# Six modulation chunks of layer 1: from TensorE products on streamed weights to row sums formed by GpSimd

## The reference

```python
mod = (jax.nn.silu(c) @ w_ada[l] + b_ada[l])[:, None, :]
sh1, sc1, gt1, sh2, sc2, gt2 = jnp.split(mod, 6, axis=-1)
h = modulate(rms_norm(x, g_mix[l]), sh1, sc1)            # h * (1 + scale) + shift
... = split_in(h @ w_in[l])                              # three token mixers and three gates
x = x + gt1 * merge_branches((o_a, o_b, o_c), (ga, gb, gc), w_branch[l], w_out[l])
x = x + gt2 * expert_choice_ffn(modulate(rms_norm(x, g_ffn[l]), sh2, sc2), ...)   # 16 experts
```

## Time and profile before

| | us |
|---|---|
| three runs | 1844.4, 1846.84, 1844.44 |
| median | 1844.44 |
| span of the profiled execution | 1846.3 |
| TensorE busy (share of the span) | 1689.6 (92%) |
| VectorE busy | 771.0 (42%) |
| ScalarE busy | 478.0 (26%) |
| GpSimd busy | 111.4 (6%) |

### The profile page before, as it was taken

One profiled execution on the slowest core, in us unless ns is written; L12 is line 12 of the kernel. 1 busy time (PEld: TensorE's weight loads), 2 busy tenths in 40 slices (PEclk: granted clock), 3 DMA queues, 4 the chain that ended last, 5 costly groups with the idle time before them and its releaser, 6 DMA issues.

```text
span 1846.3 us, 26514 instructions
## 1 busy us (share of the span) xinstructions
PE 1689.6 (92%) x10854; PEld 977.2 (53%) x10854; DVE 771.0 (42%) x1746; ACT 478.0 (26%) x1052; POOL 111.4 (6%) x149
## 2 busy tenths in 40 slices
PE   5999999999998999999898799989999997777866
PEld 2887777777674333333232398877883332222222
DVE  3455556674434233333323665577753222111111
ACT  3324455552223100000000434465441000000001
POOL 1001210000001000000000101300001000000000
PEclk8999999999998999999999999999998999999998
DMA  9532322127778999999999764337899999999996
GB/s 353 154 91 69 106 72 80 35 81 256 251 286 326 409 428 427 428 428 428 427 429 426 271 206 133 96 115 252 282 364 385 426 426 426 426 425 426 426 426 281
DMA packets 152035, 543.83 MB, mean 295 GB/s; under 512 B 10026, under 2 KB 92400, under 8 KB 126700
## 3 DMA queue, kind: packets, MB, share of 16 engines
q1 hardware_dynamic: 149104, 535.35, 74.0%
q0 software_dynamic: 2400, 6.16, 1.2%
q10 hardware_dynamic: 412, 0.64, 0.1%
HBM read 539.13 MB, written 2.98 MB: 294 GB/s over the span
## 4 chain that ended last, share of the span: by engine, by line
PE 68%; DMA 23%; DVE 4%; ACT 2%; SPq 2%; issue 1%; POOL 0%; DVEq 0%; ACTq 0%
PE bank L2158 20%; PE bank L2019 12%; PE bank L2020 11%; PE bank L2021 11%; DMA ring<-in_w_exp_down 8%; DMA ring<-in_w_exp_gate 7%; DMA ring<-in_w_exp_up 4%; DMA spare<-in_w_exp_gate 3%; PE bank L2132 2%; PE bank L2048 2%; PE bank L2071 2%; PE bank L1934 2%; PE bank L2058 2%; PE bank L2187 1%; DMA ring<-in_w_ada 1%
## 5 line engine op out<-in xcount | busy, mean ns | idle before, releaser
L2158 PE MATMUL bank<-ring,XEP 128*32 128x256 f32 (+1 forms) x2384 | 384.9, 617 | 37.1 <-DMA ring<-in_w_exp_gate 20.7
L2019 PE MATMUL bank<-HH,WH 128*128 128x512 f32 (+1 forms) x864 | 312.1, 361 | 5.7 <-DVE HL L1627 4.7
L2020 PE MATMUL bank<-HL,WH 128*128 128x512 f32 (+1 forms) x864 | 300.4, 348 | 0.0
L2021 PE MATMUL bank<-HH,WL 128*128 128x512 f32 (+1 forms) x864 | 299.9, 347 | 0.0
L2158 PEld LDWEIGHTS bank<-ring,XEP 128*32 128x32 f32 (+1 forms) x2384 | 114.1, 130 | 277.5 <-issue 227.8
L1598 DVE TENSOR_TENSOR WL<-ring,WH 128x1024 fp32r<-128x1024 f32 (+1 forms) x172 | 185.0, 1078 | 133.4 <-ACT WH L1362 132.6
L1856 DVE TENSOR_TENSOR X<-X,bank 128x512 f32<-128x512 f32 x184 | 114.0, 682 | 188.2 <-PE bank L2187 100.0
L2019 PEld LDWEIGHTS bank<-HH,WH 128*128 128x128 f32 x864 | 163.8, 190 | 54.0 <-issue 25.9
L1362 ACT CAST WH<-ring 128x1024 fp32r<-128x1024 f32 (+1 forms) x172 | 158.0, 926 | 100.5 <-PE bank L2021 64.7
L2158 PE MATMUL bank<-ring,HIDT 128*32 128x256 f32 (+1 forms) x1232 | 153.6, 481 | 31.3 <-DMA ring<-in_w_exp_down 31.3
L2021 PEld LDWEIGHTS bank<-HH,WL 128*128 128x128 f32 x864 | 163.8, 190 | 21.2
(11 more groups left out here) (244 smaller groups left out, 1955.4 us busy)
## 6 DMA issues: line engine op xcount, KB each, us to landing
ring<-in_w_exp_gate SPq DMA_DIRECT2D x55, 2048.0 KB, 30.9
ring<-in_w_exp_up SPq DMA_DIRECT2D x49, 2048.0 KB, 34.4
ring<-in_w_exp_down SPq DMA_DIRECT2D x48, 2048.0 KB, 36.6
ring<-in_w_ada SPq DMA_DIRECT2D x48, 1024.0 KB, 7.4
ring<-in_w_in SPq DMA_DIRECT2D x40, 1024.0 KB, 6.3
split_slot<-in_w_exp_up SPq DMA_DIRECT2D x8, 2048.0 KB, 29.3
split_slot<-in_w_exp_down SPq DMA_DIRECT2D x8, 2048.0 KB, 33.5
ring<-in_w_in SPq DMA_DIRECT2D x28, 512.0 KB, 5.2
```

What stands on the lines that cost most here:

```text
L2019: mm(t, wh, hi[:, k, 0:b.n], start=k == 0, stop=False)
L2020: mm(t, wh, lo[:, k, 0:b.n], start=False, stop=False)
L2021: last = mm(t, wl, hi[:, k, 0:b.n], start=False, stop=k == b.kk - 1)
L2158: last = mm(out_bank[tw * g:tw * g + tw, 0:nw], stationary(k), w[:, g::G] if spread else w[:, nw * g:nw * g + nw], start=k == 0, stop=k == ...
```

## The change

Chunks 4 to 9 of layer 1 no longer go through the ring and through step "ada". ScalarE's queue loads the halves of a chunk into `row_place`, two places of four rows of 512 columns, which are the upper halves of `X` and of `MRG` (where `spare` lies). GpSimd multiplies each row block by its value of silu(c) (one per partition, for `c` alone; the values for `c_ctx` are not needed here) and adds it to `ROWSUM`, 128 x 512. Then TensorE adds up over the partitions with four products, `ROWSUM` stationary against two columns of ones, which give the result already turned. VectorE copies eight values instead of reducing a bank.

The planner counts the dense steps. The first load stands behind step 16 of layer 1; each chunk's eight form steps begin 28 steps after its load and stand three steps apart; four steps after the last one the chunk counts as formed, and at the end of the next block its products are placed and the next load may follow. The next load waits on ScalarE, half by half, for the sums of the chunk before. The load of `spare` waits for all six chunks and stands behind the window attention, and the loads of chunk 9 are gone from there.

```diff
+ROW_AFTER, ROW_EVERY, ROW_LAG = 28, 3, 4
...
         P.add("done", blk=b)
+        if P.rows_last is not None and P.ticks - P.rows_last[0] >= ROW_LAG:
+            P.deferred.append(P.rows_last[1])
+            P.rows_last = None
...
             P.add("k", blk=atom[1], k=atom[2])
             turn_due(1)
+            form_due()
...
+    def form_due():
+
+        P.ticks += 1
+        if P.rows_due and P.ticks >= P.rows_from and (P.ticks - P.rows_from) % ROW_EVERY == 0:
+            s = P.rows_due.pop(0)
+            s.mods = P.mods
+            P.steps[P.layer].append(s)
+            if not P.rows_due:
+                P.rows_last = P.ticks, s.out_tile
+                P.rows_from = P.ticks + ROW_LAG
+        elif not P.rows_due and P.rows_left and P.ticks >= P.rows_from:
+            rows(P.layer, P.rows_left.pop(0))
...
                     run([("done", head), ("done", b)])
+                    P.rows_left = [5, 6, 7, 8, 9]
+                    rows(l, 4)
...
-        if last:
-            expert_load(Step(o_ready=("ht_ready", 2 * KD)))
...
-            if last:
-                mid = len(sums) // 2
-                now = ((4,), (5, 6), (7,), (8,))[p]
-                sums = sums[:mid] + [("call", ada(l, now[0]))] + sums[mid:] + [("call", ada(l, c)) for c in now[1:]]
             attention("sw", p, info, atoms + sums)
             info = nxt
         o_sw = P.obs
+        if last:
+            expert_load(Step(o_ready=("formed", P.formed)))
...
+                    elif s.kind == "form":
+                        w, cs = row_place[s.k // 4][:, s.k % 4, :], CS[:, s.k, 0:1].broadcast_to((128, 512))
+                        if s.k % 4 == 0:
+                            pool.wait_ge(rows_in[s.k // 4], 16 * (s.n + 1))
+                        if s.k == 0:
+                            pool.wait_ge(mod_ready, s.mods)
+                            link(nc.gpsimd.tensor_tensor(ROWSUM[:], w, cs, ALU.mult))
+                        else:
+                            link(nc.gpsimd.tensor_tensor(w, w, cs, ALU.mult))
+                            add = nc.gpsimd.tensor_tensor(ROWSUM[:], ROWSUM[:], w, ALU.add)
+                            if s.k % 4 == 3:
+                                add.then_inc(formed, 1)
+                                pool.wait_ge(formed, s.formed)
+                            else:
+                                link(add)
...
+                    elif kind == "row_load":
+                        act.wait_ge(ht_ready, KD * DEPTH)
+                        for r in range(2):
+                            if s.before:
+                                act.wait_ge(formed, s.before - 1 + r)
+                            act.dma_start(row_place[r][:], source(("w_ada", s.l, 512 * s.col, 512, 4 * r, 4))).then_inc(rows_in[r], 16)
...
+                    elif kind == "ada2" and s.formed:
+                        pe.wait_ge(formed, s.formed)
+                        for i, out_ in enumerate(s.out):
+                            t = open_tile(out_)
+                            for k in range(4):
+                                cols = slice(k, 512, 4) if i == 0 and s.v in (SH2, SC2) else slice(128 * k, 128 * k + 128)
+                                last = mm(t[:, 2 * k:2 * k + 2], ROWSUM[:, cols], SLOTS[:, 0:1].broadcast_to((128, 2)), start=True, stop=True)
+                            last.then_inc(blk_ready, 1)
```

## The result

| kernel | median, us | runs, us | ratio, 95% interval |
|---|---|---|---|
| before | 1844.42 | 1843.71 to 1846.84 | |
| after | 1884.62 | 1881.43 to 1887.2 | 1.0211, 1.0196 to 1.0225 |

The change costs 40.2 us. The forecast was 1866.8 with a range of 1841 to 1887: the direction and the place are right, the size is a little over half of what was measured. The profiled execution spans 1885.1 us, 38.8 more than the 1846.3 of before. Spans are some 2 us shorter than times (1885.1 belongs to the run of 1887.2), so the profiled execution of before took 2 to 4 us more than the medians of before on this page, and lags read against its trace look better by that than the times do.

A forecast was written before the change was run, and what follows sets the result against it. TensorE was taken to bound the dense stage and the expert stream the end. Terms -7.7 - 2.9 + 12 + 2 + 8 + 11 = +22.4 us on 1844.4 gave 1866.8 us, range 1841 to 1887.

The forecast's parts named there:

- What bounds the kernel: TensorE sets layer 1's dense stage, the expert stream the end; a microsecond on TensorE between 1050 and 1350 moves the end equally.
- Net on TensorE, -7.7: Dense stage: 14.5 us of products and transposes taken off TensorE, 64 records of 6.8 us put on; 7.7 us less.
- The start, -2.9: Layer 1's start: bias masks no longer run beside VectorE's casts and split of the normalised rows; 2.9 us gained.
- The first chunk's wait, 12 + 2: First new product: TensorE waits 12 us for late sums, then loses 2 us to half clock speed.
- the lock: GpSimd and VectorE both wanting SBUF: one stands still until the other's instruction is over; sums progress at about 60%.
- The second chunk in the convolution, 8: 1082 to 1096: GpSimd's 15 instructions put busy VectorE off; TensorE stalls 0 to 12 us, taken as 8.
- Chunks three to six, 11, bounds 0 and 20: 1129 to 1250: 60 GpSimd instructions delay VectorE's weight splits and softmax rows; 11 us, TensorE not waiting for sums.
- The range: Measured time expected between 1841 and 1887 us, 8 in 10; the forecast's own range 1846 to 1885.
- rival 3: Waits feed one another: late masks and starved weight casts make each later chunk cost 8 us; 1888 us, chance 0.13.
- ScalarE's issues at nothing: Twelve DMA issues on ScalarE, 0.37 us each, costed at nothing because ScalarE is idle over a third of every stretch.
- Rivals 1, 2 and 4: 1: all as intended, 1836, chance 0.07; 2: late sums, no lock, 1842, 0.12; 4: stage absorbs it, 1845, 0.04.

The follow-up runs named there:

- e_no_sums: Changed kernel with GpSimd's products and additions left out, except each chunk's first product and two pairs of four-column instructions; 1840.95 us.
- e_pe_free: Changed kernel with all sums in place, but TensorE does not wait for them and its product reads the identity matrix; 1881.46 us.
- e_masks_late: Kernel before, with GpSimd's first bias mask of layer 1 waiting until the split of the normalised rows is over; 1844.72 us.
- e_nobody_waits: e_pe_free with ScalarE's wait gone too: only the first chunk is loaded and its rows are summed again for the others; 1872.14 us.
- e_gpsimd_loads: Changed kernel with products at least 20 dense steps behind the sums, and GpSimd instead of ScalarE issuing the loads; 1888.78 us.
- the chunk at 1098: Second GpSimd chunk, summed 1098 to 1120, in the changed kernel with only chunks 4 and 5 on GpSimd and four on TensorE; 1857.07 us.

## Why the prediction came out as it did

**What bounds the kernel**: right. The loss is in the dense stage, 37.4 of 38.8 us between the profiled executions, and goes to the end within 1.4 us.

**Net on TensorE, -7.7**: e_no_sums has -7.7 - (-2.5) = -5.2 from step 64 to the end of the stage. The products were under-sized: all 64 records are busy for 12.5 us in the changed kernel, and for 11.3 without any wait, not 6.8. A group of eight takes 0.95 us where its weights are adjacent columns of `ROWSUM` (0.12 each, near the 0.107), and twice that where they are every fourth column, as for chunks three to six. At full clock, e_no_sums first and then e_pe_free, which reads the identity matrix in adjacent columns at the same place:

```profile
1142.28 1.91 PE L2060 MATMUL bank<-CONST,ROWSUM 128*128 128x2 f32 x8
```

```profile
1157.44 0.95 PE L2060 MATMUL bank<-CONST 128*128 128x2 f32 x8
```

Four of the eight groups are of that kind. The Trainium skill ("SBUF — State Buffer", the note on SBUF cachelines) says that accesses to the same 16-byte line go at full bandwidth and each that crosses to a new line pays; every fourth fp32 is a new line each time, and the rows agree.

**The start, -2.9**: right by the rows, 3.0 on VectorE and 3.2 on TensorE in e_masks_late, with 1.3 us in the time. The changed kernel's own 4.6 is 2.5 from step 0 on and 2.1 that was there before. The prediction took the 1846.3 us span for 1.9 above the median time; against the spans of the other runs it is some 4 above.

**The first chunk's wait, 12 + 2**: near, 11.7 for wait and clock together, with two errors that cancel. The load was issued at 1057.15, not behind the second copy at 1063, since the start gain moved it and the issue stands between the two copies; and the sums took 23.7 us (1062.34 to 1086.0) instead of 18, which is the lock at work.

**The second chunk in the convolution, 8**: near, 6.2, and e_nobody_waits shows the turns. The prediction leaned on casts, which read one matrix; the rows that show it for instructions reading two are L1725 and L1726 above.

**Chunks three to six, 11, bounds 0 and 20**: this is the step that failed. They cost 29.3. Three things were missing in it. First, the sentence that each chunk has 25 us and more, so that TensorE would not wait for sums: by the prediction's own numbers a load of 7 to 11 us and 18 us of sums are 25 to 29, as long as the period or longer. They were 5.6 and 21 to 24. GpSimd was therefore busy 60.0 of the 92 us from 1116 and 32.0 of the 42 from 1208, and TensorE waited for it at chunks three and four, 7.9 us. Second, the masks in the same queue, which made the third chunk 39.2 us long; the prediction had them only at the layer's start. Third, the clock. It was put behind one wait, 2 us; but the later stretches with waits, 1116 to 1297, were granted 0.86 to 0.95 too. The two rows beside the table of steps give the split: of the 29.3 us, 17.1 are standing and 12.2 are slower work. The term had 11 for standing and nothing for the clock, so of the 18.3 by which it fell short two thirds are the clock, and 6.1 are standing. How these divide between late sums, masks and contention was not separated.

**The range**: it held with 2.4 us to spare, and that is in part luck. This term passed its own upper bound of 20 by 9.3 us, and the sign that the prediction kept for rival 3, TensorE waiting for GpSimd at later chunks too, came true.

**ScalarE's issues at nothing**: right for the issues, wrong for the gate ahead of them. From e_nobody_waits to e_pe_free, which has the gate and the five later loads, the loss rises by 9.1 us; from there to the changed kernel, where TensorE waits as well, by 4.7, of which 3.8 are the dearer products. So of the 45.2 us that come with the sums some 35 are there with neither gate, masks' waits among them, some 9 come with ScalarE's, and about 1 with TensorE's. The parts depend on the order in which they are taken away, as e_gpsimd_loads shows, which took the gate away and won nothing.

**The rivals.** Rivals 1, 2 and 4 are out: TensorE waits, VectorE's instructions are longer, and the distance from the router's load to the end is as before. Rival 3 gave 1888 and is near in its time and in part of its mechanism (ScalarE on the next load; GpSimd later than a period), but the larger part is there without those waits, as the forecast's own lock had it.

## What to carry to other kernels

Work for GpSimd beside VectorE is not free work, even if nobody waits for it: as a first estimate, count how many VectorE instructions with SBUF operands it meets, one GpSimd instruction's length for each, as in the convolution here, and compare the sum with what VectorE has in hand in that stretch. Within it the cost was next to nothing (half the columns; the chunk at 1098); beyond it the standing reached TensorE, and about two fifths of the loss was the clock that fell with it. Then look for what waits behind the work in GpSimd's own queue, the masks here. Before moving a periodic job to another engine, add up landing, work and what else stands in that engine's queue, and hold it against the period.

## What the runs showed of the hardware

- Length matters where VectorE's instructions are short: one element took 1.22 to 1.23 us behind a GpSimd addition instead of some 0.15 to 0.22.
- An operand in PSUM spares an instruction: L1727 stayed at 0.42 in the middle of the turns, while the cast of 256 columns beside it went from 0.29 to 0.56.
- GpSimd's instructions alone are very regular: 723 ns for 256 columns of an addition, 1262 for 512, that is 2.1 ns per column and 0.19 fixed; the products with a broadcast scalar 612 and 1040, 1.67 per column. The lengthened ones reach 2.17 us.
- Weights read at every fourth column cost a small product twice the time, 1.91 instead of 0.95 us for eight records, at full clock.
- The loss is steep, not proportional: with half of GpSimd's columns the time fell by 33.4 us, to 1838.8; TensorE's standing in dense steps 80 to 360 went from 28.8 to 8.6 us and its clock stayed at 1.00.
